# Expert order by row count, and recurrence inputs made in the combining stage

## The reference, cut to what matters

```
g_idx  = top-1 of 4 groups;  top_i = top-2 of the 8 experts in that group      # per row
y[row] = sum over its 2 experts of  weight * (silu(x @ w1[e]) * (x @ w3[e])) @ w2[e]
```

## Time and profile before

| | us |
|---|---|
| three runs: median, lowest, highest | 3503.64, 3501.95, 3505.16 |
| the profiled execution's own time | 3501.22 |
| its span, first to last instruction | 3499.4 |
| PE busy in the span | 2918.9 |
| layer 0: first weight transfer of the routing phase issued, last `pY` ended | 599.05, 1156.50 |
| layer 1: the same | 1619.05, 2137.87 |
| combining: first instruction, last of ACT | 2152.05, 2210.98 |
| recurrence: first instruction, first product, first product of the next phase | 2211.25, 2218.57, 2418.20 |
| recurrence: DVE's masks, start and end | 2251.31, 2261.87 |

### The profile page before, as it was taken

One profiled execution on the slowest core, in us unless ns is written; L12 is line 12 of the kernel. 1 busy time (PEld: TensorE's weight loads), 2 busy tenths in 40 slices (PEclk: granted clock), 3 DMA queues, 4 the chain that ended last, 5 costly groups with the idle time before them and its releaser, 6 DMA issues. The chain is left out here.

```text
span 3499.4 us, 50378 instructions
## 1 busy us (share of the span) xinstructions
PE 2918.9 (83%) x20975; PEld 1625.4 (46%) x20975; DVE 1041.1 (30%) x2167; ACT 760.2 (22%) x1485; POOL 508.0 (15%) x608
## 2 busy tenths in 40 slices
PE   7998887667668598885776653799999999999999
PEld 4556654444345345653444332444444554544444
DVE  3425855211111343655111103533211331211101
ACT  2224641111112322630111112321112320111000
POOL 0003720232223001520332221000000000000000
PEclk8999998899989799996998887899999999999999
DMA  8833003999997642006999996122222111322237
GB/s 299 314 118 113 1 21 135 423 423 423 423 424 295 217 121 85 11 19 246 422 422 423 424 424 273 42 73 63 89 72 72 49 49 72 109 72 88 105 110 262
DMA packets 188522, 684.82 MB, mean 196 GB/s; under 512 B 51438, under 2 KB 92842, under 8 KB 163782
## 3 DMA queue, kind: packets, MB, share of 16 engines
q1 hardware_dynamic: 176550, 655.66, 48.1%
q0 software_dynamic: 11808, 26.78, 2.0%
HBM read 653.89 MB, written 33.98 MB: 197 GB/s over the span
## 5 line engine op out<-in xcount | busy, mean ns | idle before, releaser
L1603 PE MATMUL pH<-w,xT 128*32 128x256 f32 x7552 | 478.5, 409 | 171.2 <-DMA w<-in_moe_w 148.2
L1603 PEld LDWEIGHTS pH<-w,xT 128*32 128x32 f32 x7552 | 292.5, 118 | 338.7 <-issue 211.8
L1610 PE MATMUL pY<-w,hT 128*32 128x256 f32 x3776 | 228.2, 381 | 150.2 <-DVE hT L1641 132.9
L2646 PE MATMUL banks<-hT,wf 128*128 128x512 f32 (+2 forms) x768 | 303.2, 557 | 3.3 <-ACT hT L2703 2.8
L1639 DVE TENSOR_TENSOR hh<-hs,pH 128x128 f32<-128x128 f32 x118 | 33.9, 287 | 836.1 <-ACT hs L1622 836.1
L923 POOL TENSOR_SCALAR E<-E,st 128x768 f32<-128x768 f32 (+3 forms) x80 | 168.3, 2104 | 657.5 <-DVE st L1173 656.8
L1610 PEld LDWEIGHTS pY<-w,hT 128*32 128x32 f32 x3776 | 131.0, 109 | 247.4 <-issue 181.3
L2646 PEld LDWEIGHTS banks<-hT,wf 128*128 128x128 f32 x768 | 140.8, 190 | 164.6 <-issue 154.9
L416 PE MATMUL pa<-aT,w 128*128 128x512 f32 x416 | 206.0, 600 | 1.3 <-DVE aT L680 1.3
L2392 PE MATMUL pa<-hT,ring 128*128 128x512 f32 x384 | 167.8, 592 | 0.0
L2297 PE MATMUL pa<-hT,ring 128*128 128x512 f32 x384 | 165.0, 592 | 1.3 <-PEq L91 1.3
(11 more groups left out here) (439 smaller groups left out, 3723.2 us busy)
## 6 DMA issues: line engine op xcount, KB each, us to landing
w<-in_moe_w SPq DMA_DIRECT2D x192, 2048.0 KB
mw<-in_mod_w SPq DMA_DIRECT2D x24, 2048.0 KB, 16.4
ring<-in_w_ff_down SPq DMA_DIRECT2D x33, 1024.0 KB, 4.9
ring<-in_w_in SPq DMA_DIRECT2D x15, 2048.0 KB, 8.2
ring<-in_w_gate SPq DMA_DIRECT2D x6, 2048.0 KB, 8.5
wf<-in_w_ff_gate SPq DMA_DIRECT2D x11, 1024.0 KB, 5.7
wf<-in_w_ff_up SPq DMA_DIRECT2D x11, 1024.0 KB, 8.0
w<-in_ab_w_in SPq DMA_DIRECT2D x6, 1024.0 KB, 6.4
```

The costliest lines, as they stand in the source:

```text
L1603: last = pe.matmul(pH[strip(s), 0:2 * P].rearrange("p (j n) -> p j n", j=2), xT[:, k, :], slot_of(g, "w13", b)[:, :, k, s * P:(s + 1) * P] ...
L1610: last = pe.matmul(pY[strip(s), 0:YW], hT[:, k, :], slot_of(g, "w2", b)[:, k, s * YW:(s + 1) * YW], start=(k == 0), stop=(k == HC - 1))
L2646: last = pe.matmul(banks[f % 2][:, j * 512 + cols.start:j * 512 + cols.stop], wf[:, i % 2, j, k, (f % 2) * P:(f % 2 + 1) * P], hT[:, k, co ...
```

## The change

The order of the experts is worked out on the chip: experts 0, 1, 2 stay first; all others are ranked by their rows, most first, and position 3 + 4j + q takes a rank by a fixed rule (below, `rank_at`). SP reads the expert's number for each position from `unit_end` and addresses the weights by that register. The counts come from three products in place of 27 (nt 6) or 14 (nt 4), after nt additions on DVE; two more small products spread the order and the first blocks over the partitions. The combining phase also loads the recurrence's constants, loads ring job 1 behind tile 1's rows and job 0 behind tile 2's, and makes the value products of tiles 0 and 1 on PE (`values`), which ACT moves out (`take_values`). The recurrence makes 22 products; its masks stand at the start of DVE's list. In tiles 0 and 1 the fourth of their products is dropped, and later ones are renumbered.

```diff
 def load_gate(sp, g, l, i, e):
-        sp.dma_start(slot_of(g, "w13", b)[:, j], g[name][l, e].rearrange("(p k) n -> p k n", p=P)).then_inc(g["w13_in"][b], 16)
+        sp.dma_start(slot_of(g, "w13", b)[:, j], g[name][l, ds(e, 1)].rearrange("a (p k) n -> p (a k) n", p=P)).then_inc(g["w13_in"][b], 16)
...
 # routing_phase, POOL
+            step(pool.tensor_scalar(tie[:], key[:], -1.0, float(EARLY_SLOTS), ALU.mult, ALU.add))
+            step(pool.tensor_scalar(tie[:], tie[:], 0.0, 2.0 ** 17, ALU.max, ALU.mult))
+            pool.tensor_tensor(tie[:], tie[:], key[:], ALU.subtract)
+            step(pool.tensor_copy(rank_at[:], count[0:NE, 0:NE]))
+            n = (NE - EARLY_SLOTS) // 4
+            quarters = rank_at[:, EARLY_SLOTS:EARLY_SLOTS + 4 * n].rearrange("p (j q) -> p q j", q=4)
+            for q, (sign, first_rank) in enumerate(((-1.0, 2 * n - 1), (1.0, 2 * n), (1.0, 0), (1.0, 3 * n))):
+                pool.tensor_scalar(quarters[:, q], count[0:NE, 0:n], sign, float(EARLY_SLOTS + first_rank), ALU.mult, ALU.add).then_inc(tabled, 1)
...
 # routing_phase, PE
-            for t in range(nt + 1):
-
-                for s in range(t):
-                    last = pe.matmul(pR[:, t, :], ones[:], both[:, s, :], start=(s == 0), stop=(t == nt and s == nt - 1))
-                if t < nt:
-                    last = pe.matmul(pR[:, t, :], earlier[:], both[:, t, :], start=(t == 0), stop=True)
+            pe.matmul(pR[:, 0:nt + 1].rearrange("p a n -> p (a n)"), ones[:], upto[:].rearrange("p a n -> p (a n)"), start=True, stop=False)
+            pe.matmul(pR[:, 0:nt].rearrange("p a n -> p (a n)"), earlier[:], both[:].rearrange("p a n -> p (a n)"), start=False, stop=True)
+            last = pe.matmul(pR[0:NE, nt + 1, 0:1], upto[:, nt], ones[:, 0:1], start=True, stop=True)
             last.then_inc(ranked, 1)
+            pe.wait_ge(listed, 1)
+            pe.matmul(pL[:].rearrange("p a n -> p (a n)"), ones[0:NE, :], listing[:, 0:2].rearrange("p a n -> p (a n)"), start=True, stop=True).then_inc(placed, 1)
+            pe.wait_ge(begun, 1)
+            pe.matmul(pF[:], ones[0:NE, :], listing[:, 2], start=True, stop=True).then_inc(spread, 1)
...
 # routing_phase, DVE
+            for t in range(nt):
+                step(dve.tensor_tensor(upto[:, t + 1], upto[:, t], both[:, t], ALU.add))
...
 # expert_phase, SP
-            for i, e in enumerate(ORDER):
-                if i < EARLY_SLOTS:
-                    continue
+            for i in range(EARLY_SLOTS, NE):
+                e = sp.value_load(unit_end[0:1, NE + 1 + i:NE + 2 + i], min_val=0, max_val=NE - 1)
...
 # combine_turn_phase, SP
+                if t == 2:
+                    load_weights(sp, g, 0)
                 if t == 1:
+                    load_weights(sp, g, 1)
                     for i, x in enumerate((g["ln_g"], g["ln_b"])):
                         sp.dma_start(lrow[:, i], x[l, 1:2, :].broadcast_to([P, D])).then_inc(lrow_in, 16)
                     sp.dma_start(gcol[:], gain[0].rearrange("(p k) -> p k", p=P)).then_inc(gcol_in, 16)
-            for j in range(RING):
-                load_weights(sp, g, j)
+            sp.wait_ge(zeroed, 2)
+            # 16 constant transfers, small_in
+            sp.wait_ge(small_in, 16 * 16)
             for t in range(NLAT):
                 sp.wait_ge(h_made, t + 1)
 # combine_turn_phase, ACT
+            def take_values(t):
+                act.wait_ge(valued, t + 1)
+                act.activation(rc["gv"][:, t], pV[t][:], ACT.Copy)
...
                 weigh(t + 2)
                 root(t)
+                if t >= 2:
+                    take_values(t - 2)
 # combine_turn_phase, PE
+            def values(t):
+                pe.wait_ge(moved, t + 1)
+                pe.wait_ge(ring_in[1], loads_of(1))
+                for i in range(C):
+                    last = pe.matmul(pV[t][:], hT[:, i, tile(t)], ring[:, 1, i, :], start=(i == 0), stop=(i == C - 1))
+                last.then_inc(valued, 1)
...
                 last.then_inc(turned, 1)
+                if 1 <= t <= 2:
+                    values(t - 1)
 # recurrent_phase, PE
-            rows(4)
-            rows(5)
+            rows(6)
+            rows(7)
             pe.wait_ge(inputs, 1)
             turn_keys(0)
-            rows(6)
+            columns(8)
             turn_keys(1)
-            rows(7)
+            columns(9)
             for t in range(NLAT):
+                n = 10 + 3 * t if t < 2 else 16 + 4 * (t - 2)
                 levels(t)
-                columns(8 + 4 * t)
-                columns(9 + 4 * t)
+                columns(n)
+                columns(n + 1)
                 weigh(t)
-                columns(10 + 4 * t)
+                columns(n + 2)
                 means(t)
-                columns(11 + 4 * t)
+                if t >= 2:
+                    columns(n + 3)
```

More of the change, by code:

```diff
@@ L1293 @@
 SLOTS, EARLY_SLOTS = 4, 3
+MAGIC = 1.5 * 2 ** 23
 def units(nt):
     return NE + 2 * nt * P // UNIT
-def expert_order():
-    return [g * EPG + j for j in range(EPG) for g in range(NG)]
 def loads_before(l, i):
@@ L1453, in _ @@
             dve.wait_ge(ranked, 1)
[L1455 to L1459, removed]
+            dve.wait_ge(tabled, 4)
@@ new lines, in _ @@
+            step(dve.scalar_tensor_tensor(out=key[:], in0=counts, scalar=float(NE), in1=tie[:], op0=ALU.mult, op1=ALU.add))
+            dve.tensor_scalar(above[:], key[:, 0:NE], key[:, NE:NE + 1], None, ALU.is_gt)
+            step(dve.tensor_scalar(need[:], counts[:, NE:NE + 1], 1.0, 1.0 / UNIT, ALU.max, ALU.mult))
+            dve.tensor_reduce(by_count[:], above[:], AX.X, ALU.add)
+            step(dve.tensor_scalar(need[:], need[:], 31.0 / 64, MAGIC, ALU.add, ALU.add))
+            step(dve.tensor_scalar(need[:], need[:], MAGIC, None, ALU.subtract))
@@ new lines, in _ @@
+            dve.tensor_scalar(listing[:, 0], rank_at[:], by_count[:], need[:], ALU.is_equal, ALU.mult)
+            dve.tensor_scalar(listing[:, 1], rank_at[:], by_count[:], token[0:NE, 0:1], ALU.is_equal, ALU.mult).then_inc(listed, 1)
+            dve.tensor_scalar(above[:], rank_at[:], by_count[:], None, ALU.is_equal)
+            for k in range(2):
+                last = dve.tensor_tensor(tmp2[:, k], oh[:, k], pR[:, 0:nt, :], ALU.mult)
+            step(last)
+            for k in range(2):
+                last = dve.tensor_reduce(rank[:, k].rearrange("p (t o) -> p t o", o=1), tmp2[:, k], AX.X, ALU.add)
@@ new lines, in _ @@
+            step(last)
+            dve.wait_ge(placed, 1)
+            step(dve.tensor_copy(sequence[:], pL[:]))
+            step(dve.tensor_tensor_scan(end[:], ones[:, 0:NE], sequence[:, 0], 0.0, ALU.mult, ALU.add))
+            step(dve.tensor_tensor(first[:], end[:], sequence[:, 0], ALU.subtract))
+            step(dve.tensor_tensor(above[:], above[:], first[0:NE], ALU.mult))
+            step(dve.tensor_reduce(begin[:], above[:], AX.X, ALU.add))
+            dve.tensor_scalar(listing[:, 2], g["ident"][0:NE, 0:NE], begin[:], None, ALU.mult).then_inc(begun, 1)
@@ L1651, with combine_turn_phase @@
 DIL_W = 1536
-def combine_turn_phase(nc, g, l, share, gain, hT):
+def combine_turn_phase(nc, g, l, share, gain, hT, rc):
     with Phase(nc) as ph:
@@ L1873, in recurrent_phase @@
         product, taken = ph.sems("product"), ph.sems("taken")
-        const_in, pos_in, zeroed, masked, order, angle, tables = (
-            ph.sem(n) for n in ("const_in", "pos_in", "zeroed", "masked", "order", "angle", "tables"))
+        zeroed, order, angle, tables = (ph.sem(n) for n in ("zeroed", "order", "angle", "tables"))
         a_low, a_moved, raised, logs, rel, exped, inputs = (
```

206 lines of the change are left out of this document (112 added, 94 removed).

## The result

The changed kernel takes 3465.29 us, the median of 4 runs (3462.42 to 3467.64), beside 3504.40 for the kernel before (4 runs, 3501.95 to 3508.42): ratio 0.9887, interval 0.9870 to 0.9904. The forecast was 3443, the range to 3463, so the time lies outside it. The profiled execution took 3463.67 us, its span is 3461.9, 37.5 less than the span before; the forecast's sum was 59 less.

The account below looks back on a forecast made before the run. Weight transfers at 421 GB/s were taken to bound both expert stages. Layer 0 -43, layer 1 -5.6, combining +11 and recurrence -21.6 summed to -59 us, giving 3443 us, range 3429 to 3463.

Parts of the forecast that it names:

- End of the stage: the last w2 at 1111.5, less 1.4, and then a `pY`: Layer 0's expert stage: ends at 1113.5, shortly after the last down weights land; gain 43 us.
- PE runs without a gap here: Recurrence: PE is never idle, so dropping two products counts in full, -13.7 us.
- its first product partly at full clock: -1.4: Recurrence start: PE's first product runs partly at full clock, saving 1.4 us.
- the start (-7.3 for -7.0): Recurrence start: PE no longer waits for constants and begins at once, -7.0 us.
- `weigh(1)` (0.40 for 0.5): Recurrence, tile 1: the dropped product had been cover, so PE waits here, +0.5 us; without that cover at worst +3.
- `lrow` +4.7 (5.1): Combining: ring job 1 ahead of the normalization rows delays DVE's tile 1 and the chain behind by 5.1 us.
- values 7.08 us (7.5): Combining: the first value product on PE takes 7.5 us, with half clock for its first microsecond.
- ACT's idle 3.34 (4.0): Combining: ACT waits 4.0 us for PE's first value product, ahead of its root for tile 3.
- the rival of half clock throughout (+13): Combining: both value products run at half clock, 13 us worse, total 3456; chance 0.14.
- the blocks left behind the weights (3460): Expert stages: blocks remain behind the last weights, or the queue empties once; 15 to 20 us lost, 3460; chance 0.10.
- The register-addressed loads: Expert weight loads: reading expert number and forming address empties the queue between experts, +22 us, 3525; chance 0.04.
- the order was no empty edit: Expert order: rival that the chip in effect orders as before, leaving only -11 us, 3492; chance 0.03.

Follow-up runs that it names:

- the last version: Changed kernel with normalization rows ahead of ring job 1, value products in four halves behind the turns, ring loads 5 and 6 held until `levels` is done: 3454.96 us.
- the repeat of after: The changed kernel itself, unedited, measured and profiled once more on a second chip: 3465.92 us, ratio 0.9890 to the kernel before.
- the second half alone: Kernel before with only the new combining phase and recurrence (values and constants moved), expert order as before: 3501.86 us, ratio 0.9994.
- the rows first: Changed kernel with ring job 1 loaded behind `lrow` and `gcol` instead of ahead of them: 3463.63 us.

## Why the forecast was 22 us off

**Layer 0, 9.2 us of it: the step "End of the stage: the last w2 at 1111.5, less 1.4, and then a `pY`".** Two things in it failed. First, it took the end of the transfers from the kernel before, where PE still had 45 us of blocks ahead, whose gathers and scatters were not yet in the stream, and it spread what was in the stream over all 64 blocks. By 1111.4 that kernel had moved 13.26 MB of gathers and scatters (60 and 58 issued); the changed kernel had moved 14.89 MB by 1114.57 (66 and 65 issued). The difference of 1.63 MB is 3.9 us at 421 GB/s, and 1110.1 + 3.9 = 1114.0, against a release at 1114.57. The kernel without gathers shows that such traffic counts in full. Second, it let the last block's `pH` run before the last w2 landed. Both loads were in by the time `pH` had run, and 5.35 + 1.24 + 1.93 = 8.5 us of block stand behind 1114.57, where I had 3.4. Together 4.5 + 5.1 = 9.6. Why a few packets of w1 and w3 come so late, when most of w2 behind them is already in, is open: holding w2 back did not bring them forward.

**Layer 1, 3.2 us: the same step.** The block that went was the second behind the weights; the one left begins with w1 and w3 rather than w2, and 9.8 us stand behind that release, where before 8.6 stood behind w2's. The order's mechanism itself is right: DMA at 1.00 to 1.01 over both stages, no queue empty, one block last.

**Recurrence, 6.1 us: "PE runs without a gap here".** It does not. At two of the four `levels`, PE stands "<-issue", waiting for nothing that the profile shows, 6.2 us in all where the kernel before stood 2.8 and the forecast had no change: 3.4 us. The products right behind the stretches took 15.51 and 15.43 us, before 14.3 (without the stretch inside it) and 15.31, where they take 14.0 at full clock: 1.4 us more. And the step "its first product partly at full clock: -1.4" failed: that product took 2.79 us in place of 3.22, but the one behind it 7.92 in place of 7.13, so the two gave nothing (+0.4), 1.8 us off.

The changed kernel's second stretch, where the first window lies inside it and the second behind it:
```profile
2343.00:2346.00 3.00, 0.00 (x0) 0.00 (x0) 0.83 (x2) 0.00 (x0) 0.00 (x0) 1.00 0.95 343
2348.00:2352.00 4.00, 4.00 (x7) 1.73 (x8) 2.49 (x3) 0.79 (x3) 0.44 (x2) 0.67 0.12 47
```
and the last version's:
```profile
2341.00:2343.00 2.00, 0.00 (x0) 0.00 (x0) 1.18 (x2) 0.00 (x0) 0.00 (x0) 1.00 0.00 0
2344.00:2348.00 4.00, 4.00 (x16) 1.85 (x12) 2.50 (x3) 0.92 (x3) 0.14 (x1) 1.00 0.57 167
```
With a ring load in the DMA engines the stretch is 3.95 us and PE's clock is 0.67 afterwards; without, it is 2.26 us and the clock stays at 1.00. The clock is not lost by the long stretches alone: behind the 1.67 us of the kernel before and behind most of the first stretches (1.8 to 2.3 us) it fell to half as well, and the product there took 14.9 to 15.7 us. Around the latter stretch (2339 to 2345) the DMA view of that kernel has one queue with any packets:
```profile
q8 instruction: 2, 0.03, 2.2%
```
So I read the stretch as the fetch of instructions, which some 170 to 200 tiny products use up in 2 us. The packets of that queue bear it out: in all 28 such stretches of the thirteen traces PE goes on 2.25 to 2.71 us behind the start of a 16 KB instruction packet. In the eight long stretches (3.94 to 4.87 us) this packet starts only 1.6 to 2.5 us after PE stopped, and a ring load's packets had begun 2.0 to 3.5 us ahead of it. In the twenty short ones (1.15 to 2.53 us) it starts between 1.1 us before PE stopped and 0.2 us after; five of these had a load beside them, too, but in four of the five the load began with the packet or behind it. That holding the load back shortens the stretch is shown by three stretches in two pairs of kernels (3.95 to 2.29, 4.17 to 2.10, 4.21 to 2.13 us); that it does so because the instruction packet has to queue behind the load is argued from those times. Which `levels` a stretch falls on moved when only the order of the experts had changed, and that is open.

The other steps held: the start (-7.3 for -7.0) and `weigh(1)` (0.40 for 0.5). With the loads held back and PE arriving busy, its first product at 1.92 us, the recurrence takes 186.0 us, where the forecast's terms gave 207.0 - 21.6 = 185.4.

**Layer 1's attention, 3.0 us, in no step.** Laid on the same instruction counts, the profiles run in parallel but for two places, 122 to 144 and 212 to 230 us into it. The first place, PE's product behind its wait and a window behind that, in after:
```profile
1253.74 1.02 PE L473 MATMUL acc<-back,flip 128*128 128x448 f32 x2 [2.40 <-DVE na_bias L720]
1255.26:1258.26 3.00, 3.00 (x4) 1.15 (x4) 2.69 (x5) 0.00 (x0) 0.00 (x0) 0.50 0.00 0
```
and in the repeat of after:
```profile
1251.42 1.02 PE L473 MATMUL acc<-back,flip 128*128 128x448 f32 x2 [1.35 <-DVE na_bias L720]
1254.15:1257.15 3.00, 3.00 (x8) 1.33 (x7) 1.42 (x3) 0.00 (x0) 0.00 (x0) 1.00 0.00 0
```
After loses 3 us here: its wait is 1.05 us longer, since DVE itself waits that much longer for a store of `h`, and the clock is at half behind it. The three profiles that lose it here waited 2.4 to 3.0 us, the ten others 1.2 to 1.6, among them the kernel before. At the second place the wait is the same in all thirteen, 4.84 or 4.85 us, and behind it the clock is at half for 3.4 us or for 13.7 us: after loses nothing here, its repeat 3.2 us. The last version loses at both (460.5 us); the kernel before, the one with the second half alone, and the one with the rows first lose at neither (454.0, 454.3, 453.6). The same program falls either way. So at the first place the cause is the later store and the clock behind the longer wait; at the second only the clock differs, with nothing in the waits to explain it. Nine of the eleven profiles with an order ranked on the chip lost at least one, the two with the order before none; whether the order has a part in it is open.

**Right.** Combining came out as its chain said: `lrow` +4.7 (5.1), values 7.08 us (7.5), ACT's idle 3.34 (4.0), in all +11.4 (+11). That the sum fits so well is in part luck: tile 2's turn came 1.9 us earlier than forecast, and from there to the end of tile 3's turn it took 15.25 us in place of 12.9. And the seven profiles of this code give +11.4 to +13.9, with 7.08 to 8.27 us for the first value product. The value product ran at the full clock of 2.4 GHz nearly at once (granted clock 0.53 over 2162 to 2163, 1.00 from 2163 on). PE had stood idle for 44 us, made tile 0's turn in 4.10 us, stood 5.71 us, and made tile 1's in 4.20 us, right ahead of it. By the 7.08 us the rival of half clock throughout (+13) is out. The Trainium skill (TensorE: Matmul & The Clock Gate, Part 1) has it that half rate is the default and that activity releases it, and the trace agrees here. But the first half product of the last version, in the same phase, took 6.65 us for 8 instructions, mostly at half: it stands behind the turn of tile 0, and PE had been idle 2.27 us ahead of it. Of the other rivals, the blocks left behind the weights (3460) came nearest in time, and not in kind: no queue emptied, and no block was left but the last. The register-addressed loads cost nothing that shows (DMA 1.01), and the order was no empty edit.

## What to carry to other kernels

Where a stage is bound by transfers, take the end of the stream from all the bytes it will hold after the change, those of the work that used to follow it included, and count the whole last item of work behind the last weights, at the lower clock. Spread heavy items so that the load slots never all fill; here sorting alone was worse than no order. Look for "<-issue" beside many tiny instructions before calling an engine gapless, and keep a large load from starting just before.

## What the runs showed that I had not expected

- A burst of some 170 to 200 tiny products can leave PE without instructions for about 2 us (1.8 to 2.5 in the changed versions, 1.15 and 1.67 in the kernel before), and in eight stretches with a 2 MiB load beside it for about 4 us (3.94 to 4.87). The product behind a stretch took 14.0 to 16.3 us, the longer ones where the clock had fallen.
- The same wait of 4.85 us in layer 1's attention was followed by 3.4 us at half clock in some executions and by 13.7 us in others of the same program, 3 us of time each.
- A product right behind a turn of 4.20 us ran nearly all at full clock. One behind an idle stretch of 2.27 us, with a single turn ahead of that, ran mostly at half (6.65 us for what took 3.60 later). Which of the two conditions decided it was not tried.
- The last block of a stage is released by a few late packets: with w2 held back, the DMA engines were 64 to 78% idle in the 6 us before w1 and w3 had landed.
